# A GpSimd queue in another order: the third expert's gate and up weights ahead of its rows

## The reference

```python
def _hier_moe(x, w_gr, b_gr, w_er, b_er, w_g, w_u, w_d):
    ...
    eid = g_idx[:, None] * EXPERTS_PER_GROUP + top_i.astype(jnp.int32)
    ...
    def expert_block(args):
        xe, e = args
        return (jax.nn.silu(xe @ w_g[e]) * (xe @ w_u[e])) @ w_d[e]
    ...
```

## Time and profile before

| | |
|---|---|
| median of 3 runs | 2913.72 us |
| profiled execution, its own time | 2938.05 us |
| its span | 2936.2 us |
| TensorE matmul busy | 2679.2 us (91%) |
| VectorE busy | 1358.4 us (46%) |
| ScalarE busy | 799.8 us (27%) |
| GpSimd busy | 650.4 us (22%) |
| mean granted TensorE clock | 0.963 |
| expert stage of layer 0, first to last tanh | 1079.8 to 1417.8 us of the span |
| expert stage of layer 1, first to last tanh | 2521.1 to 2865.1 us of the span |

### The profile page before, as it was taken

How to read it: one execution, slowest core, us unless ns; L and a number is a source line. 1 busy time by engine, 2 the same in 40 slices (tenths; PEclk the granted TensorE clock), 3 DMA queues, 4 the chain that set the end, 5 groups by cost and what they waited for, 6 DMA issues and landing times.

```text
span 2936.2 us, 56004 instructions
## 1 busy us (share of the span) xinstructions
PE 2679.2 (91%) x22234; PEld 1461.6 (50%) x22234; DVE 1358.4 (46%) x3828; ACT 799.8 (27%) x1905; POOL 650.4 (22%) x664
## 2 busy tenths in 40 slices
PE   7999899999999959999599998999999996799996
PEld 4445566666655523333244456666666554233332
DVE  4213677666643542222451256677665436222224
ACT  0111355555532001111111014555555210011113
POOL 1000211111100035555310001111110000555543
PEclk9999899999999969999799999999999997899998
DMA  7212433332242539998661133334322326599975
GB/s 299 73 34 56 156 101 105 115 100 83 85 147 86 230 127 353 370 362 324 240 226 47 38 112 105 122 106 118 104 84 88 136 75 254 206 361 359 358 288 207
DMA packets 171814, 502.23 MB, mean 171 GB/s; under 512 B 48388, under 2 KB 89608, under 8 KB 146344
## 3 DMA queue, kind: packets, MB, share of 16 engines
q1 hardware_dynamic: 105624, 321.28, 31.8%
q0 software_dynamic: 50240, 120.23, 12.1%
q10 hardware_dynamic: 15696, 57.15, 4.9%
HBM read 629.15 MB, written 86.89 MB: 244 GB/s over the span
## 4 chain that ended last, share of the span: by engine, by line
PE 78%; DVE 9%; another core or an unknown queue 3%; ACT 3%; DMA 2%; issue 2%; DVEq 2%; POOL 1%; POOLq 0%; ACTq 0%; SPq 0%
PE ps L964 70%; PE ps L961 8%; ACT PT L1924 1%; DVE S_all L2972 1%; DVE grams L2470 1%; DMA xd<-o_x 1%; DMA c_x<-xd 1%; ACT S_all L2206 1%; DVEq L2973 1%; DVE krT L2995 0%; DVE negm L2974 0%; DVE uu L2470 0%; DVE t L2470 0%; DVE r_e L2470 0%
## 5 line engine op out<-in xcount | busy, mean ns | idle before, releaser
L964 PE MATMUL ps<-w_slots,xbT 128*64 128x512 f32 (+1 forms) x2048 | 460.6, 603 | 19.0 <-DVE xbT L3429 19.0
L964 PE MATMUL ps<-hT,w_in 128*128 128x512 f32 x896 | 392.0, 595 | 1.2 <-ACT hT L1924 1.2
L867 POOL DMA_INDIRECT xb<-xd,idall x256 | 256.8, 1003 | 144.7 <-issue 81.0
L964 PEld LDWEIGHTS ps<-w_slots,xbT 128*64 128x64 f32 x2048 | 144.6, 138 | 289.6 <-issue 270.4
L964 PEld LDWEIGHTS ps<-hT,w_in 128*128 128x128 f32 x896 | 167.8, 190 | 203.4 <-issue 200.0
L964 PE MATMUL ps<-w_slots,hidT 128*64 128x512 f32 (+1 forms) x1024 | 233.6, 596 | 9.4 <-issue 7.8
L964 PE MATMUL ps<-w_out,o_mixT 128*128 128x512 f32 (+1 forms) x640 | 238.3, 552 | 1.3 <-DVE o_h L3235 1.3
L3429 DVE STREAM_TRANSPOSE xbT<-xb 128x1024 f32<-128x1024 f32 x64 | 79.7, 1245 | 338.8 <-DMA xb<-xd,idall 299.5
L1924 ACT ACTIVATE kT<-ps 128x512 f32<-128x512 f32 x256 | 138.6, 593 | 127.5 <-PE ps L961 125.8
L964 PE MATMUL ps<-grams 64*64 64x64 f32 (+1 forms) x3536 | 141.1, 225 | 22.9 <-DVE grams L2470 20.9
L964 PE MATMUL ps<-kcat,qcat 96*128 96x512 f32 (+3 forms) x384 | 152.3, 505 | 8.4 <-DVE negm L2974 8.4
(11 more groups left out here) (439 smaller groups left out, 4100.6 us busy)
## 6 DMA issues: line engine op xcount, KB each, us to landing
w_slots<-in_w_gu SPq DMA_DIRECT2D x64, 2048.0 KB
w_slots<-in_w_dn SPq DMA_DIRECT2D x64, 1024.0 KB
ybd<-yb ACTq DMA_DIRECT2D x64, 512.0 KB
pd<-stage SPq DMA_DIRECT2D x56, 256.0 KB, 2.5
w_in<-in_w_in SPq DMA_DIRECT2D x6, 2048.0 KB, 24.7
out_y<-c_h ACTq DMA_DIRECT2D x18, 512.0 KB, 2.8
o_mixT<-mixd SPq DMA_DIRECT2D x18, 512.0 KB, 3.5
xd<-o_x ACTq DMA_DIRECT2D x18, 512.0 KB, 2.9
```

The source lines that it names most:

```text
L867: pool.indirect_dma_start(xb[p % 2][:, 256 * q:256 * q + 256], None, x_quarters, bass.IndirectOffsetOnAxis(ap=idall[:, NE * q + p:NE * q + ...
L964: return pe.matmul(out, lhsT, rhs, start=start, stop=stop, skip_group_check=True)
```

## The change

At the head of the expert stage's loop on GpSimd the third block (p = 2) is taken out of the loop and its fetch of gate and up weights put ahead of its rows. `dnA(l, 1)` stays behind both. The order becomes rows0, guA0, rows1, guA1, dnA0, guA2, rows2, dnA1, rows3, guA3, dnA2, rows4, ..., so that the four gathers of rows2 stand behind guA2, which waits for gu0. Nothing else is changed, and it is done in both layers.

```diff
                 rows_in(l, 1)
                 guA(l, 1)
                 dnA(l, 0)
-                for p in range(2, NE):
+                guA(l, 2)
+                rows_in(l, 2)
+                dnA(l, 1)
+                for p in range(3, NE):
                     rows_in(l, p)
                     guA(l, p)
                     dnA(l, p - 1)
```

## The result

| | before | after |
|---|---|---|
| median, 15 runs each on one chip | 2919.33 us | 2929.65 us |
| lowest and highest | 2911.65 to 2941.55 | 2920.77 to 2946.27 |
| profiled execution, its own time | 2938.05 us | 2926.92 us |
| its span | 2936.2 us | 2925.1 us |
| TensorE matmul busy | 2679.2 us | 2681.2 us |

The ratio is 1.0033 [1.0017, 1.0049]: the change costs 9.6 us (10.3 by the two medians), and 2929.65 us lies outside my range of 2906 to 2921. Of the distance to my 2914.7 us, 5.6 us are in the base alone: I started from the median of three runs, 2913.72, and over 15 runs the kernel before is at 2919.33. Yet the profiled execution of after is 11 us *shorter* than that of before.

What follows compares the result with a forecast made beforehand. TensorE was taken to bound the expert stage, so gathers count only if it waits. Only the store's 0.5 us a layer was charged: +1 us on the 2913.72 us median gave 2914.7 us, 8-in-10 range 2906 to 2921.

Steps and rivals of the forecast that it cites:

- Step 1: Fetch guA(2) on GpSimd: it waits for gu0, not the rows ahead, so it stays at 1080.59; gain nothing.
- Step 2: Block 2's rows: issued 9.0 us later, landing in 2.82 us; cost nothing, with 4.4 us of cover on TensorE.
- Step 3: Down fetch dnA(1) on GpSimd: moves from 1081.9 to 1087.1, its user dn(1) starts at 1101.12; cost nothing.
- Step 4: Block 3's rows, queued behind on GpSimd: last issued at 1092.3, block 0's eviction still 4.0 us early for dn(1) in layer 0.
- Step 5: Fetch guA(3), now landing in a loaded DMA stretch before gu3: taken as nothing, bound 1.5 us in each layer.
- Step 6: Output store of block 0, starting 2.4 us later and competing with weight loads: 0.5 us taken in each layer.
- Rival A: Block 3's last rows are caught by SyncE's loads, TensorE idles before dn(1): 6.4 us a layer, 2926.6 us; chance 0.11.
- a transpose after +20 us: Sign of Rival A: block 3's transpose starts over 20 us after guA(2), with idle TensorE before dn(1).
- Rival B: Block 2's gathers hold back gu0's end; moving them removes gaps of 3.8 and 4.3 us, 2906.6 us; chance 0.12.

Runs made afterwards that it cites:

- before_fourth: The kernel before, unchanged, run once for its profile in the fourth session: 2917.15 us.
- a: The changed kernel with dnA(1) moved ahead of guA(2), so block 3's rows come one pitch earlier: 2924.23 us, ratio 0.9996 to the kernel before.
- c: The kernel before with block 2's rows made to wait for gu0, the fetch guA(2) left behind them: 2929.39 us, ratio 1.0022.
- after_third: The changed kernel, unchanged, run once for its profile in the fourth session: 2931.69 us.
- before_again: The kernel before, unchanged, profiled in the second session: 2935.1 us, ratio 0.9987.
- before_third: The kernel before, unchanged, profiled in the third session on another chip; that session's 29 runs of it: 2935.75 us.
- b_again: The kernel of b, unchanged, in the third session: 2938.73 us, ratio 1.0014 to the kernel before.
- h: The kernel of b with block 3's rows made to wait for gu1: 2951.87 us, ratio 1.0048 to the kernel before.
- g: The kernel of b with every block's rows issued one block earlier, ahead of the fetch guA(p): 2936.62 us, ratio 0.9987 to the kernel before.
- b: The kernel before with dnA(1) moved ahead of block 2's gathers, which stay beside gu0: 2919.76 us, ratio 0.9988.
- f: The kernel before with block 2's rows put ahead of guA(1) and dnA(0), dnA(1) and guA(2) behind them: 2934.81 us, ratio 1.0046.
- after_again: The changed kernel, unchanged, in the third session: 2941.9 us, ratio 1.0011 to the kernel before.
- a_again: The kernel of a, unchanged, in the third session: 2927.61 us, ratio 0.9976 to the kernel before.
- d: The changed kernel with SyncE's load of block 5's down weights held until block 3 is transposed: 2939.08 us, ratio 0.9999 to the kernel before.

## Why the prediction was wrong

- *Step 1, the fetch.* Right that it gains nothing. That the rows ahead do not hold it up was true of the profile with the gap alone, 0.76 us behind the first tanh there and in after; without the gap (before_fourth) it was at 2.19 and 2.67 us. So the change moves it forward by 1.4 and 1.9 us, but nothing waited for it.
- *Step 2, the rows of block 2.* Right in its result. The transpose starts 8.70 us behind guA(2) instead of 8.0 (landing 3.48 us, not 2.82); the transposes of block 1 on TensorE still start without idle.
- *Step 3, dnA(1).* Right that nothing waits for it. But its 1.30 us stand ahead of block 3's rows, and a shows that this one pitch decides whether they are late. The step should have said so.
- *Step 4, the rows of block 3: the step that failed.* Their last issue came where I put it: 1088.01, 11.73 us behind guA(2), nine pitches. Two terms were wrong.
  - **The load's place.** I counted 13.35 us from guA(2) to the load (1080.59 to 1093.94) and 20.5 us to dn(1). Both came from a profile in which block 1 ran at a low clock behind the gap: 11.99 us for records that otherwise take 10.45. Without it the load comes 11.57 us behind guA(2), and dn(1) is wanted at 18.91 us (1095.19). "1.6 us ahead of the load" became 0.16 us behind it.
  - **The landing time.** I took 2.82 us with 6.62 as far bound. Behind the load it was 8.04 and 6.90 us, and 7.12 to 9.55 in c and after_third. The 6.62 us were no bound: that gather was issued 6.0 us behind its load (1099.94 against 1093.94 in the earlier trace rows), when most of it had moved, and not at its start. From transpose to dn(1) are 2.03 us, so what would still have done is 18.91 - 11.73 - 2.03 = 5.15 us. 8.04 - 5.15 = 2.89, the idle time in the chain.
- *Step 5, guA(3).* gu3 follows without idle (1103.89 in the chain), but there it is late for another reason. In a, where dn(1) is on time, gu3 waits for this fetch, 0.29 and 0.67 us: the term that I took as nothing is real, and below my bound of 1.5.
- *Step 6, the store.* The 0.5 us is not there. Block 1's eviction in layer 0 waits for TensorE, not for the store. In layer 1 it waits for the store, and gu3 does not wait for it.
- *Rival A* is what happened, in mechanism and place; I gave it 0.11. My 6.4 us a layer was 2.1 to 7.0 us, since in after the transpose ended 9.45 us behind the load's issue, where I had 11.4 (1105.3 - 1093.94). My argument against it, "two thirds of the wait lie in an idle stretch", was true of the slower block 1 alone. Its sign, a transpose after +20 us, came at +19.77, for the same reason.
- *Rival B* is, as far as can be told, not what was timed. The gap is absent in before_fourth although block 2's gathers are beside gu0, and the timed runs of the first result (2919.33 us) stand where those of the sessions without it do; a timed run itself has no trace. In sessions that have the gap, it does leave gu0 once the rows are moved, so part of B was right there.

The 24 us by which the profile stood above the runs was in my text, and I carried it "unscaled" without asking where it lay. It lay partly in the very place I was pricing: two gaps of 3.8 and 4.3 us and 1.5 and 1.1 us of slower matmuls make 10.7 us, of the 20.9 us between that profile and before_fourth.

## What to carry to other kernels

When a small gather shares the DMA engines with bulk loads, look at which is issued first, not at the load on average: in these profiles a gather 1.1 us ahead of a 3 MB burst landed in 2.8 us, one 0.16 us behind it in 6.9 to 9.6. Whether that costs anything hangs on what its consumer has to spare: 8.5 us cost block 2 of before_fourth nothing. So for each moved gather, find the next bulk load and take its distance with TensorE at the clock it normally has. And if the profiled execution stands far off the timed runs, find those microseconds before you build a sum on any distance in it.

## What the hardware showed that I had not expected

**A late signal of TensorE in some sessions.** The timeline of before_again:

```profile
1064.73 9.45 PE L964 MATMUL ps<-w_slots,xbT 128*64 128x512 f32 x32 [9.46 <-DVE xbT L3429]
...
1077.90 0.38 ACT L2412 ACTIVATE gt<-ps 128x256 f32<-128x256 f32 x1 [40.45 <-remote]
```

gu0's records end at 1074.18, yet ScalarE starts at 1077.90, 3.7 us later, and SyncE and GpSimd with it. Across the profiles this gap is 3.7 to 5.8 us. TensorE idles in it, its granted clock falls behind it (0.58 in the earlier trace rows), and the 48 records after it take 12.01 us in before_again where they take 10.45 without a gap: over 5 us a layer. All profiles of kernels whose block 2 gathers lie beside gu0 have it in the second and third session (before_again, before_third, b_again, h, g), none in the first and fourth (b, f, before_fourth). Medians of the kernel before were 2937.44 and 2935.75 us in the sessions with it, 2920.55 and 2922.45 in those without; the first result's 2919.33 is like the latter, though the profile of before that stands beside it has the gap. One chip was in both kinds, so it isn't the chip alone. With the rows behind gu0 a gap of 2.7 to 4.2 us shows at dn0 instead, beside block 3's gathers (after_again, a_again, d). Why gathers beside a group of matmuls should go with it isn't shown. What makes a session of one kind or the other, and whether the rest of the some 15 us between these medians is the same thing elsewhere, stays open. So does the change's worth there: 1.0011 [0.9994, 1.0029] is no difference that can be told.

**A fetch that moves nothing still waits behind a load.** In f it landed some 8 us after its issue, behind 2 MB of weights; in layer 0 of the same profile, issued 1.30 us ahead of them, it held nothing up.
